# Two steps later in the weight groups: the turned gate columns and the linear attention of a hybrid block

## The reference, cut to what matters

```python
def gla_chunkwise(q, k, v, log_alpha):
...
    def step(state, chunk):
        qx, kx, vx, la = chunk
        bcum = jnp.cumsum(la, axis=1)
...
        att = jnp.einsum('bthd,bjhd,btjhd->bhtj', qx, kx, decay)
        o_intra = jnp.einsum('bhtj,bjhv->bthv', att, vx)
        o_inter = jnp.einsum('bthd,bhdv->bthv', qx * jnp.exp(bcum), state)
        btot = bcum[:, -1]
        k_dec = kx * jnp.exp(btot[:, None] - bcum)
        state_new = jnp.exp(btot)[..., None] * state + jnp.einsum('bjhd,bjhv->bhdv', k_dec, vx)
        return state_new, o_intra + o_inter
...
def hybrid_layer(x, norm_g, w_in, b_gates, conv_w, w_alpha, b_alpha, rel_bias, ml_norm_g, gla_norm_g, w_out):
...
    qk = jax.nn.silu(causal_conv(jnp.concatenate([mq, mk], axis=-1), conv_w))
...
    h_ml = mlstm_chunkwise(mq_c.reshape(bsz, s, ML_HEADS, HEAD_DIM), mk_c.reshape(bsz, s, ML_HEADS, HEAD_DIM),
                           mv.reshape(bsz, s, ML_HEADS, HEAD_DIM),
                           mi + b_gates[:ML_HEADS], mf + b_gates[ML_HEADS:])
```

## Time and profile before

| what | value |
|---|---|
| median of 3 runs | 2014.38 us (2013.98 to 2023.43) |
| the profiled execution: time | 2020.27 us |
| the profiled execution: span | 2018.6 us |
| TensorE busy | 1888.4 us, 94% |
| VectorE busy | 1575.8 us, 78% |
| ScalarE busy | 1213.7 us, 60% |
| GpSimd busy | 437.6 us, 22% |
| mean granted TensorE clock | 0.965 |

### The profile page before, as it was taken

The page is one execution under the profiler, slowest core; times in us unless marked ns, Lnnn a source line. Parts: engine busy times, 40 slices in busy tenths (PEclk is TensorE's granted clock), DMA queues, the critical chain, the costliest instruction groups (busy, mean ns, idle before and its releaser), DMA issues.

```text
span 2018.6 us, 27084 instructions
## 1 busy us (share of the span) xinstructions
PE 1888.4 (94%) x9331; PEld 1504.9 (75%) x9331; DVE 1575.8 (78%) x1614; ACT 1213.7 (60%) x1246; POOL 437.6 (22%) x381
## 2 busy tenths in 40 slices
PE   6999998787999797899999999999999999999997
PEld 5766655575677676788888888888888888888884
DVE  5763344584356749889999999999999999999996
ACT  5545555432446342267777777777777777777773
POOL 4435533002016062061111111111111111111110
PEclk9989987998999898799999999999999999999998
DMA  7435440505200133499999999999999999999994
GB/s 207 160 104 188 136 141 27 203 9 116 63 11 10 30 97 110 172 318 347 399 390 399 390 399 385 395 385 397 394 385 394 387 392 379 399 390 391 394 368 146
DMA packets 180402, 525.06 MB, mean 260 GB/s; under 512 B 34531, under 2 KB 52019, under 8 KB 180339
## 3 DMA queue, kind: packets, MB, share of 16 engines
q1 hardware_dynamic: 156882, 458.27, 59.9%
q0 software_dynamic: 21376, 65.95, 11.3%
q10 hardware_dynamic: 2080, 0.01, 0.1%
HBM read 499.06 MB, written 25.12 MB: 260 GB/s over the span
## 4 chain that ended last, share of the span: by engine, by line
PE 56%; DVE 1%; DMA 1%; issue 0%; SPq 0%; POOL 0%; POOLq 0%; DVEq 0%
PE banks L3386 52%; PE banks L3374 3%; DMA bias_rows<-bias_parts 1%; PE banks L3380 1%; PE banks L3450 0%; DVE expert_weights L3724 0%; DVE x_tokens L3720 0%; SPq L3145 0%; DVE x_tokens L3731 0%; SPq L3245 0%; PE banks L3507 0%; PE banks L3471 0%; DVE u_lo L3556 0%; DVE less_mean L3722 0%; DVE inverse_root L3730 0%
## 5 line engine op out<-in xcount | busy, mean ns | idle before, releaser
L3520 DVE TENSOR_TENSOR weights_lo<-expert_weights,weights_hi 128x2048 fp32r<-128x2048 f32 x384 | 876.7, 2288 | 65.9 <-ACT weights_hi L3760 61.9
L3760 ACT ACTIVATE weights_hi<-expert_weights 128x2048 fp32r<-128x2048 f32 x384 | 738.8, 1926 | 264.7 <-PE banks L3386 249.6
L3386 PE MATMUL banks<-weights_hi,rows_hi 128*128 128x512 f32 x1024 | 319.1, 393 | 0.0
L3386 PE MATMUL banks<-weights_hi,rows_lo 128*128 128x512 f32 x1024 | 315.5, 389 | 0.0
L3386 PE MATMUL banks<-weights_lo,rows_hi 128*128 128x512 f32 x1024 | 273.8, 389 | 0.0
L3386 PEld LDWEIGHTS banks<-weights_hi,rows_hi 128*128 128x128 f32 x1024 | 189.8, 188 | 44.9 <-issue 7.3
L3386 PEld LDWEIGHTS banks<-weights_hi,rows_lo 128*128 128x128 f32 x1024 | 192.3, 188 | 40.4
L3386 PEld LDWEIGHTS banks<-weights_lo,rows_hi 128*128 128x128 f32 x1024 | 192.3, 188 | 39.9
L3386 PE MATMUL banks<-weights_hi,u_hi 128*128 128x512 f32 x512 | 161.8, 397 | 1.4 <-DVE u_lo L3556 1.4
L3386 PE MATMUL banks<-weights_hi,u_lo 128*128 128x512 f32 x512 | 158.7, 391 | 0.0
L3386 PE MATMUL banks<-weights_lo,u_hi 128*128 128x512 f32 x512 | 136.9, 389 | 0.0
(11 more groups left out here) (594 smaller groups left out, 2774.2 us busy)
## 6 DMA issues: line engine op xcount, KB each, us to landing
expert_weights<-in_exp_w SPq DMA_DIRECT2D x384, 1024.0 KB, 10.6
enter_rows<-in_ada_w POOLq DMA_DIRECT2D x24, 1024.0 KB, 5.7
w_in_landing<-in_w_in SPq DMA_DIRECT2D x16, 384.0 KB, 3.3
second_landing<-in_w_in SPq DMA_DIRECT2D x12, 512.0 KB, 3.6
x_tokens<-in_x SPq DMA_DIRECT2D x8, 512.0 KB, 6.5
w_in_landing<-in_w_in SPq DMA_DIRECT2D x8, 512.0 KB, 3.6
enter_w_landing<-in_w_out SPq DMA_DIRECT2D x8, 512.0 KB, 5.4
rwkv_room<-in_w_o SPq DMA_DIRECT2D x8, 512.0 KB, 8.0
```

Of the source, the lines that this page charges most:

```text
L3386: last = nc.tensor.matmul(c.banks[:, bank + n, :], left[:, 2 * q + kk, :], right[:, q, kk * FF + n * 512:kk * FF + (n + 1) * 512], start=s ...
L3520: nc.vector.tensor_tensor(w_lo[:, ch % SPLIT, :], c.raw[:, ch % RAW if place is None else place, :], w_hi[:, ch % SPLIT, :], ALU.subtract) ...
L3760: nc.scalar.activation(w_hi[:, ch % SPLIT, :], c.raw[:, ch % RAW if place is None else place, :], ACT.Copy).then_inc(hi_ready.sem, 1)
```

## The change

`cols_at` is two steps more, 52 instead of 50, and with it, since they are counted from it, `tile_at` (58, 60, 62, 64), all that hangs on either, on all engines. The convolution, the mLSTM, the pieces of the weights and the partition sums keep their steps. No instruction is added or taken away.

```diff
@@ -409,7 +409,7 @@
     pieces, end = 4 * len(groups), len(quarters)
     RAWS, PLACES, ROW = 2, 3, 32
 
-    gates_at, cols_at = first[2], first[3] + 2
+    gates_at, cols_at = first[2], first[3] + 4
     tile_at = [cols_at + 6 + 2 * t for t in range(TT)]
     units = [(h, j) for h in range(H) for j in range(TT)]
     NM = len(units)
```

## The result

| | before | after |
|---|---|---|
| median (lowest to highest) of 22 runs each | 2014.34 us (2010.38 to 2023.43) | 2019.89 us (2010.14 to 2029.11) |
| ratio, 95% interval | | 1.0029 [1.0016, 1.0042] |
| profiled execution: time, span | 2020.27, 2018.6 us | 2027.24, 2025.6 us |
| mean granted TensorE clock in it | 0.965 | 0.960 |

The change costs 0.3%: within the 0.5% that the forecast took as no difference, 4.8 us above the forecast of 2015.1 and inside its range, but the interval lies clear of 1. So small as it is, it has to be explained.

A forecast was written before the change was run, and what follows sets the result against it. TensorE's order was taken to pace the changed stretch, its three waits (7.4 us) being what could be won. Idle became 7.2 us, but two more steps at low clock made L758 0.7 us later: 2014.38 plus 0.7 gives 2015.1 us, range 2007 to 2022.

The forecast's parts named there:

- no difference of 0.5%: Whole kernel: time stays within 0.5% (10 us), chance 0.80; faster 0.10, slower 0.10.
- Step 1: Gate columns, m=50 to m=52: m=51 runs first, the 3.80 us wait shrinks to 2.0 us on GpSimd before L809.
- ScalarE no longer late: At the moved columns: GpSimd's addition, ending at 100.9 us, is late next, not ScalarE.
- Step 2: Keys, m=57: convolution delayed 3.7 us by turn-taking with GpSimd; keys ready at 119.4 us, TensorE idle 5.2 us.
- Rival A: VectorE's third convolution: GpSimd's addition comes at another moment or VectorE gets through first; block 3 to 5 us earlier; chance 0.18.
- Step 3: First scores, m=58: the 2.65 us wait is gone, covered by slow m=58; scores and first state product take 2.4 us.
- Step 4: Rest up to the first mLSTM score: 24.1 us less 3.2 us, so L758 at 146.0 us, 0.7 us later.
- Step 5: Edits costed at nothing: last linear output, ScalarE's copies, low parts ahead of masks; some 3 us of cover.
- rival B: Last mask, behind piece 18's low part: comes late, deciding from 2 us on; then 3 to 5 us, about 2019; chance 0.11.
- I carry a shift of the block's end one to one into the end: From first block's end to kernel's end: nothing of the next block runs ahead, so 0.7 us is added unchanged.
- rival C: Attention steps, 240 to 345 us: shift changes granted clock; slower, about 2026, chance 0.09, or faster, 2004, chance 0.08.

The follow-up runs named there:

- Experiment 4: Changed kernel with ScalarE's `exps` one step later, so that the copy L874 stands ahead of it: 2021.01 us, ratio 1.0029.
- experiment 2: Changed kernel with the third convolution part two steps later, behind the scaling of the keys: 2018.87 us, ratio 1.0016.
- the two of before: Kernel before, profiled at 2020.27 us, and the same kernel once more without any edit: 2014.25 us, ratio 0.9994.
- experiments 5 and 7: Kernel before with small products repeated three times ahead of the second block's scores, 2019.95 us; kernel before with 20 unread products in the first block's attention, 2013.24 us.
- experiments 2 to 4: Changed kernel with third convolution part two steps later, 2018.87 us; columns moved one step instead of two, 2021.22 us; changed kernel with `exps` one step later, 2021.01 us.
- the filled ones: Changed kernel with six unread products in the second block's scores stage, 2018.62 us; with these and 20 in the first block's attention, 2012.91 us.
- the repeat: Changed kernel once more without any edit: 2019.86 us, ratio 1.0018.
- the delayed changed kernel: Changed kernel with two small products repeated twice ahead of the second block's scores: 2017.47 us, ratio 1.0014.

## Why the prediction was right, and where it wasn't

The forecast "no difference of 0.5%" held; the local mechanism was right in kind, but its sign wasn't: 0.7 us later was forecast for L758, and it came 1.2 us earlier. That the time still came out within 5 us is partly luck, as the loss arose where the forecast had none. Step by step:

- *Step 1, the columns: wrong cause.* It had TensorE do m=51 at once and wait 2.0 us for GpSimd before L809. But m=51 writes the fourth bank, and this is freed by ScalarE's L874, which stands behind the five activations of `exps` (L927 to L932). So the wait for `exps` stayed: 4.19 us, before the products. In the earlier trace rows L715's wait for L932 had covered it. Experiment 4 shows this: with L874 ahead of `exps` the 2.1 us on L636 appear. "ScalarE no longer late" was the error: I followed the semaphore that L715 waits for and not the bank that the step moved in front of it needs.
- *Step 2, the keys: right, sizes off by little.* Convolution 6.0 us (forecast 6.5), keys ready at 118.7 (119.4), wait 4.0 (5.2). Rival A, the free port, is out: wherever I put the convolution (experiment 2), VectorE's work beside GpSimd's two additions was stretched by 3.2 us: 6.0 for 2.8 us of convolution, 6.00 for 2.77 of scalings, and before, 2.2 at L1126 and 1.0 at L1064. The exclusive lock that the Trainium skill describes ("SBUF — State Buffer", "SBUF: two separate sides") fits every one of these rows. It names VectorE instructions with two SBUF inputs, as L1066, L1122 and L1126 are, and those in a two-port mode; L1064 has one tensor input and can only be of the second kind, which no row shows.
- *Step 3: right on the wait, wrong on the clock.* No wait before L729, but I had its products at the low clock, 2.4 us; they took 1.1 (122.02 to 123.12).
- *Step 4: right.* From the end of these products to L758, 20.9 us forecast and 21.0 measured. The 2.0 us by which L758 came sooner than forecast (144.1, not 146.0) are 0.6 of step 2, 0.1 and 1.3 of step 3.
- *Step 5 and rival B: right.* No wait for a mask, though L1153 met a GpSimd addition (134.36 to 136.75 us) and took 2.02 us where a tile before it took 0.36:

```profile
130.68 0.36 DVE L1153 TENSOR_SCALAR mixer_room<-mixer_room,gla_carry 128x256 f32<-128x256 f32 x1
...
134.88 2.02 DVE L1153 TENSOR_SCALAR mixer_room<-mixer_room,gla_carry 128x256 f32<-128x256 f32 x1
```

- *"I carry a shift of the block's end one to one into the end": the step that failed.* The stretch ended 1.2 us early and the kernel 5.6 us late by the medians. In the traces 7.8 us are won back in the first block's attention, by the clock, and 17.0 us are lost in the second's, 15.8 of them by the clock and 1.2 by the longer wait. The clock's part is rival C, to which I gave 0.17; but I had it only between 240 and 345 us, where it helped this execution, and not behind 600 us. There and the profile before show a full clock, which I took as safe.

The longer wait, unlike the clock, goes with the order of the first block in every trace. In the four traces of the order of before that have no fill in this stage (the two of before, experiments 5 and 7) TensorE waits 0.27 or 0.28 us at this place; in the six of the moved orders (the two of the changed kernel, experiments 2 to 4, and 5) it waits 1.51 or 1.52 us, whether the clock falls or not. This L2465 lasts 0.70 us in all five traces of the one order and 1.68 or 1.69 us in all eight of the other, the filled ones too. What decides is who starts first, VectorE's L2465 or GpSimd's L2287, and VectorE comes late because an L2447 ahead of it starts some 0.3 us later in all eight (behind 0.80 us of idle time, not 0.44 or 0.45), with TensorE's and GpSimd's rows ahead of it at the same distances. What holds this L2447 up, no row shows. Where the low stretch occurs it begins within 0.8 us behind the end of this wait: in four of the six traces with 1.52 us, in none with less.

How much of the medians' 5.6 us is this? Runs of before (the 111 of which the clock is known) and of the changed kernel (33), sorted by their mean granted clock:

| granted clock | before: runs, mean us | after: runs, mean us |
|---|---|---|
| up to 0.961 | 11, 2023.3 | 8, 2028.2 |
| 0.962 to 0.963 | 18, 2020.6 | 7, 2021.0 |
| 0.964 to 0.965 | 31, 2016.2 | 6, 2020.3 |
| 0.966 to 0.967 | 20, 2014.5 | 7, 2017.3 |
| 0.968 and more | 31, 2011.3 | 5, 2012.6 |

All in all the means are 2015.9 and 2020.6 us at clocks of 0.9655 and 0.9638. A line through all single runs gives 1.3 us (before) and 1.5 us (after) for a thousandth of clock, so the 0.0017 carry 2.2 to 2.6 us of the 4.7, about half; the rest stays at equal clock, above all in the lowest class. The longer wait is 1.2 us of that rest: in the traces without a low stretch and without a fill the scores' stage lasts 55.5 and 55.9 us in the changed kernel and 54.3 to 54.7 in those before. **What stays open:** what makes L2447 late in the second block, whether the wait of 1.52 us alone makes the low stretch behind 600 us likely, and the last 1 us at equal clock. All three traces of runs above 2025 us (the changed kernel, one step, `exps` later) have 38 us of it, experiment 2's has 17, and none of the five traces of the kernel before and its variants has any; but two traces have the wait and no low stretch (the repeat and the delayed changed kernel), no run puts the wait of 1.52 us into the kernel before, and runs that weren't profiled show only their mean clock.

## What to carry to other kernels

When a wait is moved behind another step, look up what that step itself waits for, its PSUM bank as much as its inputs: a wait that covered another one gives it back. Two waits in a row on different engines are one budget: removing one of them (experiments 2 and 4) left the end of the stretch within 0.3 us. And where a kernel has stages that alternate short products with short waits, a local shift isn't carried one to one to the end; look at the granted clock and the waits of every later stage in several executions, before and after, ere a few tenths of a per cent are ascribed to the edit. A wait that is the same in every trace of one order and different in every trace of the other belongs to the edit, even in code that it doesn't touch.

## What the runs showed of the hardware that I hadn't expected

- TensorE's clock stayed at 1.2 GHz for 38 us while TensorE was busy for 48 of 50 us. It fell behind a wait of 1.52 us in four of six traces; in the other two the same wait left it at 2.4 GHz, as one of 0.27 us did in all four that have it. The price was 15.8 us on a stage of 55.9.
- A lead of 0.13 us decides which of two instructions of VectorE and GpSimd runs through: L2465 took 0.70 us when it started first and 1.68 to 1.69 us when GpSimd's L2287 did, in 13 traces of 13.
- Products whose results nobody reads needn't cost time: with 20 of them the low time between the first L758 and L1443 was 21 and 12 us in the two traces, against 22 to 44 us in the eleven others, and the time of the kernel wasn't longer for it (both ratios 0.9985, their intervals reaching 1).
- The mean granted clock of a run orders the times of one and the same kernel: 2023.3 us at up to 0.961 and 2011.3 us from 0.968 on, with not one instruction different.
